# Gathering both rows of a PEER expert at once, and working them off pair by pair

## The reference, cut to what matters

```python
q = (xb @ w_q).reshape(T, 8, 2, 128)
s = jnp.einsum('thpd,hpnd->thpn', q, keys)          # two lists of 128 scores per head
sv, si = lax.top_k(s, 16)                           # best 16 of each list
cand = sv[:, :, 0, :, None] + sv[:, :, 1, None, :]  # 256 sums
cv, ci = lax.top_k(cand, 16)                        # best 16 sums
eid = si1[ci // 16] * 128 + si2[ci % 16]
g = softmax(cv)
u = jnp.take(u_tab, eid, axis=0)                    # rows of 1024 f32
act = gelu(einsum('thkd,td->thk', u, xb))           # 128 dots per token
out = einsum('thk,thkd->td', g * act, jnp.take(v_tab, eid, axis=0))
```

## Time and profile before

| what | value |
|---|---|
| median of the runs | 2397.8 us (2373.89 to 2413.68) |
| span of the profiled execution | 2391.5 us, 17018 instructions |
| what lies around the span, by the median | 6.3 us |
| DVE busy | 1553.8 us (65%) |
| POOL busy | 1365.4 us (57%) |
| PE busy | 1361.7 us (57%) |
| ACT busy | 259.0 us (11%) |
| HBM read | 618.95 MB, 260 GB/s over the span |

### The profile page before, as it was taken

One profiled execution on the slowest core, in us unless ns is written; L12 is line 12 of the kernel. 1 busy time (PEld: TensorE's weight loads), 2 busy tenths in 40 slices (PEclk: granted clock), 3 DMA queues, 4 the chain that ended last, 5 costly groups with the idle time before them and its releaser, 6 DMA issues.

```text
span 2391.5 us, 17018 instructions
## 1 busy us (share of the span) xinstructions
PE 1361.7 (57%) x4280; PEld 756.2 (32%) x4280; DVE 1553.8 (65%) x2987; ACT 259.0 (11%) x571; POOL 1365.4 (57%) x1170
## 2 busy tenths in 40 slices
PE   6899999989998100466660036666003666000776
PEld 2565865546887100122250012225001222000222
DVE  2545056666128888767688876658887665898444
ACT  1201110002121000111110011111001111000111
POOL 2488003212005677665677766668776667777775
PEclk9899899999999655788885578998556989555999
DMA  9234111113466788888898888899888889999998
GB/s 319 83 130 159 53 34 37 53 53 112 153 194 226 267 278 266 301 318 303 318 365 321 294 329 298 318 338 347 318 316 324 300 318 332 374 405 368 399 363 323
DMA packets 214219, 622.24 MB, mean 260 GB/s; under 512 B 19325, under 2 KB 76901, under 8 KB 214117
## 3 DMA queue, kind: packets, MB, share of 16 engines
q0 software_dynamic: 152608, 556.86, 64.1%
q1 hardware_dynamic: 59296, 61.94, 8.2%
q10 hardware_dynamic: 2212, 2.32, 0.3%
HBM read 618.95 MB, written 2.10 MB: 260 GB/s over the span
## 4 chain that ended last, share of the span: by engine, by line
issue 25%; DVE 16%; DMA 15%; POOL 10%; PE 4%; POOLq 1%; ACT 0%; DVEq 0%; ACTq 0%
DMA arena<-in_peer_v,arena 12%; POOL arena L508 10%; DVE arena L1421 6%; PE bank L760 4%; DMA arena<-in_peer_u,arena 3%; DVE arena L1472 2%; DVE arena L1354 1%; DVE arena L1346 1%; DVE arena L1342 1%; DVE arena L1338 1%; DVE arena L1350 1%; DVE arena L1364 0%; POOLq L502 0%; DVE arena L1381 0%; DVE arena L1377 0%
## 5 line engine op out<-in xcount | busy, mean ns | idle before, releaser
L760 PE MATMUL bank<-arena 128*128 128x512 f32 x1024 | 548.6, 668 | 864.1 <-ACT arena L1003 642.8
L508 POOL DMA_INDIRECT arena<-in_peer_u,arena x512 | 610.0, 1191 | 375.9 <-issue 151.5
L508 POOL DMA_INDIRECT arena<-in_peer_v,arena x512 | 550.6, 1075 | 257.4 <-issue 123.7
L1421 DVE CUSTOM_DVE_ANT_0 arena<-arena 128x1024 f32<-128x1024 f32 x512 | 618.8, 1225 | 107.3 <-DMA arena<-in_peer_u,arena 96.8
L760 PEld LDWEIGHTS bank<-arena 128*128 128x128 f32 x1024 | 194.6, 209 | 1216.4 <-issue 974.4
L1472 DVE SCALAR_TENSOR_TENSOR arena<-arena 128x1024 f32<-128x1024 f32 x252 | 323.8, 1285 | 294.2 <-DMA arena<-in_peer_v,arena 287.9
L568 PE MATMUL bank<-arena 128*128 128x512 f32 (+1 forms) x832 | 327.2, 551 | 3.5 <-ACT arena L841 3.3
L568 PEld LDWEIGHTS bank<-arena 128*128 128x128 f32 x832 | 158.3, 192 | 154.7 <-issue 145.5
L1003 ACT ACTIVATE arena<-ident,arena 128x128 f32<-128x128 f32 x256 | 101.6, 401 | 660.1 <-PE bank L760 658.3
L789 PE MATMUL bank<-arena 128*128 128x256 f32 x512 | 121.7, 399 | 14.3 <-ACT arena L958 14.3
L740 PE MATMUL bank<-arena 128*128 128x256 f32 x512 | 110.7, 379 | 1.5 <-issue 1.5
(11 more groups left out here) (226 smaller groups left out, 1321.7 us busy)
## 6 DMA issues: line engine op xcount, KB each, us to landing
arena<-in_w_in SPq DMA_DIRECT2D x24, 1024.0 KB, 5.6
arena<-in_w_ada POOLq DMA_DIRECT2D x16, 1024.0 KB, 5.9
arena<-in_w_out SPq DMA_DIRECT2D x16, 1024.0 KB, 5.0
arena<-in_w_ada SPq DMA_DIRECT2D x8, 1024.0 KB, 11.3
arena<-in_peer_w_q SPq DMA_DIRECT2D x8, 1024.0 KB, 6.7
arena<-in_peer_u,arena POOLq DMA_INDIRECT x512, 6.1
arena<-in_peer_v,arena POOLq DMA_INDIRECT x512, 6.2
arena<-in_x SPq DMA_DIRECT2D x4, 512.0 KB, 12.4
```

The lines of the kernel that those rows point to most:

```text
L508: nc.gpsimd.indirect_dma_start(gslot[n % NGS], None, tab, bass.IndirectOffsetOnAxis(eid[:, k:k + 1], 0)).then_inc(s_gsl[n % NGS], 16)
L760: last = mm(acc[h][:, :], diag[:, i % NDG], gslot[s][:, h * 512:(h + 1) * 512], start=(i == 0), stop=(i == NPE - 1))
L1421: V.tensor_tensor_reduce(gslot[s], gslot[s], h2c, 1.0, 0.0, ALU.mult, ALU.add, dots[:, k:k + 1]).then_inc(s_used, 1)
```

## The change: what it does

The host lays `u_tab` and `v_tab` side by side as one table of rows of 8 KB (`peer_uv`). One gather brings a `u` row and its `v` row for 128 tokens: 512 gathers of 1 MB in place of 1024 of 512 KB. The slots are six of 8 KB per partition in place of eight of 4 KB. A list `BSEQ` sets the order on every engine: for each pair of rows `j` (256 in all)

- DVE makes both dots, then up to four steps of the ranking, then adds the even `v` row, for which it waits for ACT's weight (`s_wexp`);
- ACT makes the gelu of the two dots, then two weights, then the diagonal of the odd row;
- PE adds the odd `v` row;
- POOL waits for the adder of the even slot or PE for the odd slot.

The ranking takes two heads at a time (a group, 16 pairs of rows for 32 rows), as a generator that gives four instructions a pair for the first 12 of 16 pairs (`rank`), and its ids go out per group. Only the first two heads are ranked ahead of the first dot. The query products of all blocks are cut into three steps a unit (four lists), one step behind each of the first 42 pairs; PE's and ACT's query work is thus put between the rows. The gates' exponentials (`gates`) come once per group, the square root of the final norm between pairs. Output goes out through SP. Row sums in PSUM are copied by ACT (`products`), and `h2`, `scur`, `kTt`, `h2T` get other places in SBUF. The loop is written out.

```diff
+    for j in range(NBT):
+        if j and j % BT == 0:
+            BSEQ.append(("vs", j // BT - 1))
+        BSEQ.append(("pk", j))
+        if j in (0, 2):
+            BSEQ.append(("h2T", 2 + j // 2))
+        u = 2 + j // 3
+        if u < len(units):
+            BSEQ += unit_steps(units[u])[j % 3]
...
-        gslot = [at(100 + 4 * n, D) for n in range(6)] + [at(180 + 4 * n, D) for n in range(2)]
+        gslot = [at(k, 2 * D) for k in (56, 64, 72, 80, 100, 108)]
...
+            for n in range(NPK):
+                t, k = n // NE, n % NE
+                if n % TOP == 0:
+                    h = n // TOP
+                    pool.wait_ge(s_eid, h + 1 if h < 2 else h // 2 + 2)
+                if n >= NGS:
+                    if n % 2:
+                        pool.wait_ge(s_peused, (n - NGS) // 2 + 1)
+                    else:
+                        pool.wait_ge(s_vadd, (n - NGS) // 2 + 1)
+                nc.gpsimd.indirect_dma_start(
+                    gslot[n % NGS], None, uv_tab[0], bass.IndirectOffsetOnAxis(eid[t % 2][:, k:k + 1], 0)
+                ).then_inc(s_gsl[n % NGS], 16)
...
+            def add_row(j):
+                pe.wait_ge(s_diag, j + 1)
+                landed(pe, n)
+                for h in range(2):
+                    last = mm(acc[h][:, :], diag[:, j % NDG], row_v(n)[:, h * 512:(h + 1) * 512],
+                              start=(i == 0), stop=(i == BT - 1))
...
-                A(wexp, dots, ACT.Gelu_apprx_tanh).then_inc(s_gelu, 1)
+            def pick(j):
+                t, k = j // BT, 2 * j % NE
+                act.wait_ge(s_dot, 2 * j + 2)
+                A(gelu[:, k:k + 2], dots[:, k:k + 2], ACT.Gelu_apprx_tanh).then_inc(s_gelu, 1)
+                act.wait_ge(s_gelu, j + 1)
+                h = 2 * j // TOP
+                act.wait_ge(s_gready, h + 1 if h < 2 else h // 2 + 2)
+                for i in range(2):
+                    A(wexp[:, k + i:k + i + 1], gate[t % 2][:, k + i:k + i + 1], ACT.Copy,
+                      scale=gelu[:, k + i:k + i + 1]).then_inc(s_wexp, 1)
+                act.wait_ge(s_wexp, 2 * j + 2)
+                if j >= NDG:
+                    act.wait_ge(s_peused, j - NDG + 1)
+                A(diag[:, j % NDG], ident[:], ACT.Copy, scale=wexp[:, k + 1:k + 2]).then_inc(s_diag, 1)
...
+            def pick(j):
+                for n in (2 * j, 2 * j + 1):
+                    landed(dve, n)
+                    k = n % NE
+                    V.tensor_tensor_reduce(row_u(n), row_u(n), h2[:, t], 1.0, 0.0, ALU.mult, ALU.add,
+                                           dots[:, k:k + 1]).then_inc(s_dot, 1)
+                g = j // BP + 2
+                if j % BP < 12 and g < len(groups):
+                    if j % BP == 0:
+                        ranking = rank(g)
+                    for _ in range(4):
+                        next(ranking, None)
+                n = 2 * j
+                w = wexp[:, n % NE:n % NE + 1]
+                dve.wait_ge(s_wexp, n + 1)
...
+                    dve.wait_ge(s_vadd, j)
+                    V.scalar_tensor_tensor(out=vacc, in0=row_v(n), scalar=w, in1=vacc,
+                                           op0=ALU.mult, op1=ALU.add).then_inc(s_vadd, 1)
```

More of the change, by code:

```diff
@@ L128, in build @@
     plan += [("kT", q4) for q4 in range(NQ // 4)]
[L129 to L137, removed]
+    place = {name: (n % NBANK, n // NBANK) for n, name in enumerate(plan)}
@@ new lines, in build, with unit_steps @@
+    assert len(place) == len(plan)
+    NPK = LT * NE
+    NBT = NPK // 2
+    BT = NE // 2
+    BP = TOP
+    QB = NQ // 4
+    units = [(0, 0), (0, 1), (1, 0), (2, 0), (3, 0), (1, 1), (0, 2), (2, 1), (3, 1), (1, 2), (0, 3),
+             (2, 2), (3, 2), (1, 3), (2, 3), (3, 3)]
+    assert len(set(units)) == LT * QB
+    groups = [(0, 0, (0,)), (0, 0, (1,))]
+    groups += [(n // QB, n % QB, (0, 1)) for n in range(1, LT * QB)]
+    def unit_steps(u):
+        return [[("q", *u, 0)], [("q", *u, 1)], [("qT", *u), ("s", *u)]]
@@ new lines, in build @@
+    BSEQ = [("h2T", 0)] + sum(unit_steps(units[0]), []) + [("rank", 0), ("norm", 0), ("rank", 1), ("norm", 1)]
+    BSEQ += [("h2T", 1)] + sum(unit_steps(units[1]), [])
+    for j in range(NBT):
[8 more added lines that the diff above has]
+        g = j // BP + 2
+        if g < len(groups):
+            if j % BP == 11:
+                BSEQ.append(("rank", g))
+            if j % BP == 12:
+                BSEQ.append(("norm", g))
+        if j >= BT and j % BT in (0, 1, 3, 4):
+            BSEQ.append(("fin", j // BT - 1, (0, 1, 3, 4).index(j % BT)))
@@ new lines, in build @@
+    BSEQ.append(("vs", LT - 1))
+    BSEQ += [("fin", LT - 1, n) for n in range(4)]
+    used = [sum(b == i for b, _ in place.values()) for i in range(NBANK)]
+    qring = []
+    for step in BSEQ:
+        if step[0] == "h2T":
+            qring += [("h2T", step[1], h) for h in range(2)]
+        elif step[0] == "q" and step[3] == 0:
+            qring.append(step[:3])
+        elif step[0] in ("qT", "s"):
+            qring.append(step)
+    for n, name in enumerate(qring):
+        place[name] = (n % 4, used[n % 4] + n // 4)
@@ L139, in build @@
+    for t in range(LT):
+        for h in range(2):
+            b = 4 + 2 * (t % 2) + h
+            place["vs", t, h] = (b, used[b] + t // 2)
     with ExitStack() as stack:
@@ L344, in build @@
         wq_0 = len(loads)
-        for n in range(WRING):
-            add_load(w_q[0], 0, n, None)
+        for n in range(2 * QB):
+            last = [u for u in units if u[1] == n // 2][-1]
+            add_load(w_q[0], 0, n, ("q", *last))
         block = stack.enter_context(nc.Block())
@@ L989, in gates @@
[L989 to L1012 removed]
+                    if u >= 2:
+                        await_filled(act, ("qT", *units[u - 2]))
@@ L1015, in _ @@
+            parts = {"h2T": queries_T, "q": query_half, "qT": query_T, "s": scores, "rank": gates,
+                     "pk": pick, "vs": products, "fin": finish}
+            for kind, *n in BSEQ:
+                if kind in parts:
+                    parts[kind](*n)
         @block.vector
```

565 lines of the change are left out of this document (241 added, 324 removed).

## The result

| | us | runs |
|---|---|---|
| kernel before | 2392.92 (2373.89 to 2413.68) | 4 |
| changed kernel | 2148.65 (2145.29 to 2152.75) | 4 |
| ratio | 0.8988, 95% interval 0.8942 to 0.9033 | |

A forecast was written before the change was run, and what follows sets the result against it. It took underfilled DMA engines, starved by packed DVE work, as the bound. 729.3 + 10 + 273 + 1166 + 9 + 12 gave a span of 2199 us, 192 less than before, hence 2206 us; range 2135 to 2300.

The forecast's parts named there:

- the mixture: Row stage: spreading DVE's dots, weighted rows and ranking evenly keeps the DMA engines full; 267 us to win, less its costs.
- 214 pairs at 5.45 us: Pairs after the query stretch: DMA sets the pace at 385 GB/s, 1166 us in all.
- fast memory: Pairs after the query stretch: longer pieces move at 407 GB/s, 5.15 us a pair, 2142 us in total; chance 0.14.
- The first 42 pairs: Pairs with query work: ACT's order and waits for PE make 6.5 us a pair, 273 us in all.
- The kinds of pair: Query stretch, units of three pairs: 5.0, 7.6 and 6.9 us by the query step behind each, together 19.5 us.
- ACT's reply: After a pair's second dot: DVE idles 0.82 us for gelu and weight, showing in 6 of 16 pairs.
- my sum of 4.90 us a pair: DVE's dots, weighted row, ranking, ACT wait and table load per pair; below DMA's 5.45, with 0.55 us in hand.
- Start and end: First gather at 729.3, first dots 10 us later; 12 us at the end for copies, adds and the root's table.
- Slow memory: Pairs after the query stretch: gathers move at 368 GB/s, 5.70 us a pair, 2260 us in total; chance 0.17.
- C: Gather slots: only three pairs in flight limit the pace, up to 2300 us in the range; chance 0.14.
- DVE and ACT: Row loop: ACT's reply of 1.6 us shows in every pair, 6.1 us a pair, 2345 us in total; chance 0.06.
- Slower than before (E): POOL's issue grows with the bytes: 3.5 us a gather over 512 gathers, 2550 us in total; chance 0.04.

The follow-up runs named there:

- the split: Changed kernel with each 1 MB gather issued as two of 512 KB, 1024 issues in all: 2415.17 us, ratio 1.0069 to the kernel before.
- the far halves: Changed kernel with gathers in two 4 KB pieces, dots and sums over 256 columns, second piece from another expert's row: 2152.34 us.
- the late copies: Changed kernel with ACT's query-product copies behind the next pair's gelu, weights and diagonal, and PE's scores one pair later: 2113.57 us.
- short DVE: Changed kernel with DVE's dots and weighted rows over 256 of 1024 columns: 2118.65 us.
- no ranking: Changed kernel with the ranking left out from the third group on, earlier ids and gates used again: 2118.4 us.
- four slots: Changed kernel with four slots of 1 MB instead of six, so two pairs in flight: 2503.16 us.
- the last kernel: Changed kernel with the late copies, plus the last four 1 MB query-weight loads made two of 2 MB in 2 KB pieces: 2092.6 us.

## Why the prediction was right, and where not

**The direction was right, the mechanism in part.** That ranking starved the queue is shown: taking it away gave 161 us before and 30 after. But I had put the whole gain on the mixture, and the split shows that the mixture alone gives none: it has no phase in which POOL is left alone at 0.95 us, so with 1024 issues POOL sets 6.4 us a pair. What the forecast's account left out is the issue itself. Between 985 and 2030 the kernel before spent 720.5 us on 636 issues and 172.4 on the gaps behind them, 893 of 1045 us; the issues of 1.99 us beside packed dots, which I had read as a main cause, were few (43 of the 888 issues from 985 to 2380 took 1.8 us or more, 551 under 1.0). The change also halves the number of issues, and my sum took that for granted without giving it a price. So it is in part luck that the forecast came out in direction and size.

**The mis-sized term is the pace of the transfers: 214 pairs at 5.45 us.** They took 5.18 (from the row at 1032.9 to the last one at 2135.61, 213 steps), 58 us less in all. I read the share of 1.00 in the last block as the DMA engines' own limit. It was near POOL's. In the window at 2060 POOL issued 233 gathers in 320 us, 1.37 us each. Its groups there:

```profile
L508 POOL DMA_INDIRECT arena<-in_peer_v,arena x128 | 134.3, 1049 | 41.1 <-issue 25.9 <-PE bank L760 13.1 <-DVE arena L1472 2.1
L508 POOL DMA_INDIRECT arena<-in_peer_u,arena x105 | 108.3, 1031 | 33.0 <-issue 31.7 <-DVE arena L1421 1.3
```

Mean issues of 1.03 and 1.05 and an idle time before them that is mostly the 0.30 of "issue": others kept POOL waiting for 16.5 of the 320 us. With the far halves the engines take 4 KB pieces at 405 GB/s and the share reads 1.02. So a share of 1.00 does not say that the engines cannot do more. The rival "fast memory", with 5.15 us a pair, named exactly this argument (POOL's own limit, gone when a gather carries twice as much) and got 0.14. It should have had more than the forecast. Its 2142 us is 7 off, but that is closer than its working: with the span it is 2135 against 2149.2. It has 20 us too little for the start and the first 42 pairs and 11 too much for the turns and the end.

**The first 42 pairs** took 6.86 us each, forecast 6.5: 288 us in place of 273. The kinds of pair were mis-sized: 4.9, 9.1 and 6.6 us in the mean, where I had 5.0, 7.6 and 6.9. The middle kind is the one of the timeline at 861. What came before it, on PE and ACT:

```profile
855.52 4.08 PE L806 MATMUL bank<-arena 128*128 128x256 f32 x16
...
856.20 0.40 ACT L1046 ACTIVATE smalls<-ident,arena 128x128 f32<-128x128 f32 x1
...
859.44 1.88 PE L835 MATMUL bank<-arena,smalls 128*128 128x512 f32 x4
```

I had let PE begin the row as soon as its diagonal is ready, at 856.60. But the first half of the query product, begun behind the pair before, kept PE until 859.44: 2.8 us that my sum for this kind lacks. ACT is idle 8.22 us before the copy and everything behind it in line waits. The place and the mechanism (ACT in order, held by PE) were as forecast, and the late copies show it: 41 us less with that order alone, 56 us less by the medians when the weights came in time too (on other chips; by the ratios to the kernel before, 0.8988 became 0.8683).

**ACT's reply** leaves DVE idle 0.60 us, forecast 0.82 for two instructions and their handoffs. **DVE** had time in hand as forecast: it was hidden behind the transfers, but not wholly. By my sum of 4.90 us a pair nothing of it should have shown; short DVE and no ranking each give 30 us, so DVE still costs some 0.14 us a pair (an estimate, 30 us over 213 pairs); which wait carries it was not followed.

**Start and end.** The first gather starts at 731.17 (forecast 729.3), the first dot at 739.5, 10 us after 729.3 as forecast. The last even row ends at 2136.9 and the store is issued at 2146.54: 9.6 us, forecast 12. Around the span lie 1.8 us (2150.96 and 2149.2 of the same execution), not the 6.3 that I took from a span and a median of different executions. The pairs at the three turns between blocks take 9.18, 7.68 and 7.67 us, but the pairs beside them make it up: the stretches that hold the last two (64 to 128, 128 to 192) run at 5.18 and 5.22 like their neighbours, and the forecast's 9 us left no trace in the sum.

**The sum again**, with measured terms: the first weighted row starts at 744.6 (the forecast let the 42 pairs begin at 739.3), 42 x 6.86 = 288, 213 x 5.18 = 1103, the last row's 1.3 and 9.6 at the end: 2146.5, where the store's issue ends; the span is 2149.2.

**The rivals.** Fast memory is what happened in size. Slow memory (5.70) did not. The slots were enough, by the estimate above with 2 us in hand. No run shows the loop over the slots of 13 to 15.8 us that the expectation for four slots reckons with, nor the 2300 us that the range gives to C; four slots turned over in 13.6 us. PE's rows took 1.98 to 3.78 us for four products. (The clock around reads 1.00 from 1540 on, 0.65 in the row at 1549.86, 0.71 in the 8.3 us behind it and 1.00 again from 1561.5.) POOL waited 150.9 us for PE in all, yet the share stayed at 1.00. DVE and ACT did not become the bound outside the query stretch. Slower than before (E) did not come: an issue of 8 KB rows takes 1.37 us in the mean and 0.94 at the least, so its cost does not grow with the bytes. What it does grow with is DVE's work beside it. Two issues out of the changed kernel's timeline, the first beside two dots (1.68 us), the second beside steps of the ranking of 0.1 to 0.3 us each (0.94 us):

```profile
867.42 1.68 POOL L550 DMA_INDIRECT arena<-in_peer_uv,arena  x1 [4.88 <-DVE arena L1501]
...
869.41 0.94 POOL L550 DMA_INDIRECT arena<-in_peer_uv,arena  x1 [0.30 <-issue]
```

The length of a DVE instruction alone does not do it. A step of the ranking that reads one input of 1024 columns (L1453) is as long as a dot, and an issue within it is not stretched, while one beside a weighted row and the dots behind it takes three times as long:

```profile
1108.78 1.22 DVE L1453 TENSOR_REDUCE smalls<-arena 128x64 f32<-128x1024 f32 x1
1108.83 0.94 POOL L550 DMA_INDIRECT arena<-in_peer_uv,arena  x1 [0.30 <-issue]
...
1158.32 1.28 DVE L1501 SCALAR_TENSOR_TENSOR arena<-arena 128x1024 f32<-128x1024 f32 x1
1158.47 3.08 POOL L550 DMA_INDIRECT arena<-in_peer_uv,arena  x1 [0.30 <-issue]
1159.51 1.22 DVE L1486 CUSTOM_DVE_ANT_0 arena<-arena 128x1024 f32<-128x1024 f32 x1
```

All 12 issues that began within such a step between 1100 and 2120 took 0.94 or 0.95 us. The step also writes only 64 columns, so these rows do not tell reading from writing. With short dots and rows the mean of the split kernel's issues falls from 1.30 to 0.98. The stretching cost little here, at most the 30 us of the run with short DVE, since two issues fit in a pair, and 267 us where four had to (2415.17 against 2148.32, on two chips).

## What to carry to other kernels

A queue that is fed by one engine can have that engine's issue rate as its limit, as here with four issues of 1.30 + 0.30 us in a pair of 6.4: divide the bytes of an issue by its duration plus its gap before you call a pace the memory's, and make each issue carry more if they agree. Heavy work on the side cost much here in whole heads of 8.8 us (161 us) and little once it was spread in small pieces among work that the transfers pace (30 us). In an engine that works in order, put the small reply that others wait for ahead of the copy that waits for a long product (41 us here).

## What the runs showed of the hardware that was not expected

- One core alone moves 406 GB/s of gathered rows for 1020 us, 416 with DVE busy 43% of the time and 417 at 75% (no ranking); pieces of 4 KB reach 405 and 406 when their issue keeps up, as 8 KB rows do beside full DVE work.
- The profile's DMA share reads 1.00 at 385 GB/s and 1.00 to 1.02 at 406 to 416. It is no measure of what is left.
- A gather's issue on POOL costs the same 0.94 to 0.95 us for rows of 4 KB and of 8 KB, and up to 3.08 beside dots and weighted rows, which read two inputs of 1024 columns; a reduction of 1.22 us with one such input and 64 columns of output leaves it at 0.94 to 0.95.
- Beside gathers of 8 KB pieces a weight load of 1 MB in 1 KB pieces takes 32.9 us (median of four) from issue to landing, where it takes 5.3 before they begin (the first four in the last kernel). In the changed kernel, whose gathers moved 314 to 328 GB/s there, the same four loads took 17.9 (median). Two loads of 2 MB in 2 KB pieces took 27.4.
- PE's granted clock is 0.74 of full speed in the mean of the long stretch; it was 0.50 from 1452.7 to 1456.6 and 1.00 from 1457.93 to 1460. A row of four products takes from 1.98 to 3.78 us, and the idle time just before it does not tell which: after 1.39 us without work one took 1.98 (at 1457.93) and another 3.78 (at 1452.76).
